# Turning the delta rows by a transposing DMA, with ScalarE's order and the first expert loads moved

## The reference, cut to what matters

```python
h = concat([meta, x])                                  # 4112 rows of 1024
u = rmsnorm(h, mix_norm)
proj = u @ w_in                                        # 3080 columns: xb, gb, q, k, v, z, beta, a
y_lru = rmsnorm(rglru(conv(xb)) * gelu(gb))            # 512 wide, a recurrence over the tokens
y_dn  = rmsnorm(gated_deltanet(q, k, v, beta, a)) * silu(z)   # 4 heads of 128, a recurrence over chunks
h = h + concat([y_lru, y_dn]) @ w_out
logits = rmsnorm(h, ffn_norm) @ router                 # top-1 of 4 groups, top-2 of its 8 experts
h = h + sum over the two chosen experts of gate * (silu(x @ w_gate) * (x @ w_up)) @ w_down
out = rmsnorm(h, final_norm)[16:]
```

## Time and profile before

| | |
|---|---|
| median of 3 runs | 3208.48 us (3200.05 to 3215.45) |
| the profiled execution | 3197.16 us, of which span 3195.5 us |
| TensorE busy | 2935.7 us (92% of the span) |
| VectorE, ScalarE, GpSimd busy | 2554.9, 1973.5, 907.7 us |
| mean granted TensorE clock | 0.969 of full speed |

### The profile page before, as it was taken

The page is one execution under the profiler, slowest core; times in us unless marked ns, Lnnn a source line. Parts: engine busy times, 40 slices in busy tenths (PEclk is TensorE's granted clock), DMA queues, the critical chain, the costliest instruction groups (busy, mean ns, idle before and its releaser), DMA issues. The chain is left out here.

```text
span 3195.5 us, 81737 instructions
## 1 busy us (share of the span) xinstructions
PE 2935.7 (92%) x28640; PEld 2195.9 (69%) x28641; DVE 2554.9 (80%) x7201; ACT 1973.5 (62%) x4385; POOL 907.7 (28%) x962
## 2 busy tenths in 40 slices
PE   4788999999999999999999999996799999999960
PEld 4777888788878887888788888874344555554530
DVE  6887888888878887888788878876788888888844
ACT  7554666565656566656555565653677777777746
POOL 4422222122212222221222122212344444444420
PEclk9999999999999999999999999998899999999985
DMA  6111232322222222222222222225487877777749
GB/s 231 65 37 32 70 100 72 86 71 75 74 87 68 81 74 81 68 81 76 79 74 74 82 73 80 70 72 211 119 275 223 239 211 199 193 222 217 230 99 394
DMA packets 186113, 396.53 MB, mean 124 GB/s; under 512 B 86992, under 2 KB 86992, under 8 KB 173520
## 3 DMA queue, kind: packets, MB, share of 16 engines
q1 hardware_dynamic: 148896, 286.22, 26.6%
q0 software_dynamic: 29216, 89.30, 12.2%
q10 hardware_dynamic: 7696, 16.86, 1.4%
HBM read 280.05 MB, written 96.01 MB: 118 GB/s over the span
## 5 line engine op out<-in xcount | busy, mean ns | idle before, releaser
L621 PE MATMUL pj<-uT,W 128*128 128x128 f16 x15744 | 974.4, 220 | 12.3 <-POOL W L1939 12.3
L621 PEld LDWEIGHTS pj<-uT,W 128*128 128x128 f16 x15744 | 927.0, 98 | 40.7 <-issue 30.4
L2295 DVE SCALAR_TENSOR_TENSOR W<-W,ecol 128x512 f16<-128x512 f16 x664 | 447.4, 746 | 111.0 <-ACT W L2239 103.1
L2239 ACT ACTIVATE W<-W,ecol 128x512 f16 x664 | 415.8, 708 | 79.2 <-issue 77.0
L2203 PE MATMUL bA<-W,uT 128*128 128x512 f16 x1992 | 447.1, 381 | 5.6 <-issue 4.4
L2203 PEld LDWEIGHTS bA<-W,uT 128*128 128x128 f16 x1992 | 193.6, 98 | 229.1 <-issue 10.0
L2187 PE MATMUL pj<-W,qs 128*128 x664 | 299.8, 594 | 0.9 <-ACT qs L2266 0.9
L2000 POOL TENSOR_TENSOR decb<-upto,nbeta 128x512 f32<-128x512 f16 x33 | 36.1, 1093 | 889.7 <-DVE nbeta L1735 889.7
L1025 ACT ACTIVATE ht<-ht 128x512 f32<-128x512 f32 x256 | 159.2, 623 | 95.2 <-DMA ht<-w_up 89.9
L2187 PEld LDWEIGHTS pj<-W,qs 128*128 128x128 f32 x664 | 119.9, 190 | 120.8 <-issue 120.2
L1055 ACT ACTIVATE qh<-bA 128x256 f32<-128x256 f32 x198 | 76.8, 388 | 191.4 <-PE bA L787 187.7
(11 more groups left out here) (508 smaller groups left out, 6119.8 us busy)
## 6 DMA issues: line engine op xcount, KB each, us to landing
ht<-w_gate SPq DMA_DIRECT2D x128, 256.0 KB, 3.1
ht<-w_up SPq DMA_DIRECT2D x128, 256.0 KB, 3.2
W<-w_gate SPq DMA_DIRECT2D x32, 1024.0 KB
W<-w_up SPq DMA_DIRECT2D x32, 1024.0 KB
W<-w_down SPq DMA_DIRECT2D x32, 1024.0 KB
x_in<-xm SPq DMA_DIRECT2D x33, 512.0 KB, 4.5
ht<-xm SPq DMA_DIRECT2D x32, 512.0 KB, 3.8
h_rows<-ht SPq DMA_DIRECT2D x32, 512.0 KB
```

Source lines behind the costliest of these rows:

```text
L621: mm = pe.matmul(pj[g % 2][:, j, :], w16[:, k, w_half(w_high, COL[GROUPS[g]], 512, j * P, P)], (ul if low_u else uh)[:, k, :], start=(k == ...
L2239: nc.scalar.activation(part_of(wx[par][:, 0], k), raw[:, k], ACT.Copy, scale=ecol[par][:, k:k + 1]).then_inc(sem("wx_high"), 1)
L2295: a = nc.vector.scalar_tensor_tensor(out=part_of(wx[par][:, 1], k), in0=raw[:, k], scalar=ecol[par][:, k:k + 1], in1=part_of(wx[par][:, 0] ...
```

## The change

The delta rows are split into halves before they are turned: ScalarE writes the high half from `yt` into `yd_rows`, a float16 view of the tile `ks`; VectorE the low half beside it; and one transposing DMA on SP's queue (`delta_columns`) turns both into `yd16`. TensorE's `turn_delta` is gone. VectorE waits for the DMA before the convolution of k overwrites `ks`. In steps with raw chunks the DMA stands ahead of chunk 2, elsewhere behind the `u_rows` store.

On ScalarE the copy of turned values moves ahead of the second norm's rsqrt and the evacuation of `xb`, and the square of chunk 1 (in steps 0 and 4, chunk 3) moves behind `level_y(s, 5)`. Step 32 now loads only expert 0; experts 1 to 3 are loaded in step 33.

```diff
+        yd_rows = ks[:].rearrange("p j n -> p (j n)").bitcast(F16)
...
# SP
                         for c in range(KT):
                             if c == KT - 2 and n == 1:
                                 turned_rows(s)
+                            if c == 2 and n == 0:
+                                delta_columns(s)
...
+                def delta_columns(s):
+                    if s.O:
+                        need(sp, sem("yd_ready"), s.nO)
+                        sp.dma_start(yd16.rearrange("p s j n -> p (s j) n"), yd_rows, transpose=True).then_inc(sem("yd_full"), 16)
...
                     raw_chunks(s)
+                    if not s.sums:
+                        delta_columns(s)
...
                             sp.wait_ge(sem("ba_full"), TILES)
-                            for slot in range(WSLOTS):
+                            load_expert(sp, 0, 0)
+                        if isinstance(s.i, int) and s.i == TILES:
+                            for slot in range(1, WSLOTS):
                                 load_expert(sp, slot, slot)
# TensorE
                         if j == 4:
-                            need(pe, sem("yd_ready"), s.nO)
+                            need(pe, sem("yd_full"), 16 * s.nO)
...
-                def turn_delta(s):
-                    need(pe, sem("yt_ready"), s.nO)
-                    need(pe, sem("kd_ready"), s.nG)
-                    for h in range(H):
-                        mm = pe.transpose(bT[:, h, :], yt[:, h, :], ident[:])
-                    mm.then_inc(sem("yd_full"), 1)
...
                     level_x(s, 3)
-                    if s.O and s.G:
-                        turn_delta(s)
...
-                        turn_delta(s)
                     late_part(s, 2)
                     if s.G:
                         need(pe, sem("X_new"), 6 * s.pG + 5)
-                        need(pe, sem("yd_ready"), s.nO)
+                        need(pe, sem("kd_ready"), s.nG)
# ScalarE
                         nc.scalar.activation(junk[:], ht[:], ACT.Square, accum_out=hst[:, 0:1]).then_inc(sem("h_stat"), 1)
+                    if s.G:
+                        need(act, sem("pre_full"), 5 * s.pG + 3)
+                        need(act, sem("vn_full"), s.pG)
+                        nc.scalar.activation(vt[:], bC[:], ACT.Copy).then_inc(sem("vt_ready"), 1)
+                    if s.R:
                         need(act, sem("h_stat"), 2 * s.pR + 1)
                         rsqrt(hst[:, 0:1], hst[:, 1:2], 1.0 / D, eps[:], ("h_stat", 2 * s.nR), "h_norm")
                     evac(s, 0, "xb")
                     if s.G:
-                        need(act, sem("pre_full"), 5 * s.pG + 3)
-                        need(act, sem("vn_full"), s.pG)
-                        nc.scalar.activation(vt[:], bC[:], ACT.Copy).then_inc(sem("vt_ready"), 1)
...
                     if s.O:
-                        need(act, sem("yd_full"), s.nO)
-                        nc.scalar.activation(yd16[:, 0], bT[:], ACT.Copy).then_inc(sem("yd_high"), 1)
+                        need(act, sem("yt_ready"), s.nO)
+                        nc.scalar.activation(yd_rows[:, 0:512], flat(yt), ACT.Copy).then_inc(sem("yd_high"), 1)
...
-                    if s.G:
-                        raw_squares(s, 1, twice=(3,))
                     level_y(s, 5)
                     if s.G:
-                        raw_squares(s, twice=(4,))
+                        raw_squares(s, 1, twice=(3, 4))
# VectorE
                     need(dve, sem("yd_high"), s.nO)
-                    nc.vector.tensor_tensor(yd16[:, 1], bT[:], yd16[:, 0], ALU.subtract).then_inc(sem("yd_ready"), 1)
+                    nc.vector.tensor_tensor(yd_rows[:, 512:1024], flat(yt), yd_rows[:, 0:512], ALU.subtract).then_inc(sem("yd_ready"), 1)
...
                     level_x(s, 6)
+                    if s.P:
+                        need(dve, sem("yd_full"), 16 * s.nO)
                     conv(s, 2, ks, 0, 1, 2, 3)
```

## The result

The changed kernel takes 3219.88 us (median of 7 runs, 3215.09 to 3225.53) where the kernel before takes 3204.39 us (7 runs, 3199.51 to 3215.45): the ratio is 1.004, 95% interval [1.0026, 1.0054]. That is 8 to 17 us more, where 8 us less was forecast; the forecast's median was 3201 and its widest range 3181 to 3215. The profiled execution has a span of 3218.4 us, 22.9 more than the one before.

What follows compares the result with a forecast made beforehand. TensorE's sequence of starts was taken to bound steps 3 to 31. Terms -12.2 - 8.4 - 8.1 + 5 + 16 = -7.7 us gave a 3201 us median; range 3188 to 3211, with rivals 3181 to 3215.

Steps and rivals of the forecast that it cites:

- step 4: ScalarE and TensorE wait as chunk 2 is loaded only after the delta rows: 5 us once, bounds 3 and 7.
- the three gains: TensorE's savings at the turned values, delta-row transposes and fifth level: 28.7 us together, about 0.95 a step, ends 18 and 34.
- Rival 2: In the levels the next wait replaces the removed ones; a step gains only 0.45 us: 3215 us, chance 0.10.
- `vt`: Ahead of `bC<-St,kh`: moving ScalarE's copy of turned values up removes 0.38 us in 32 steps, 12.2 us.
- The turn: At the fourth level: dropping TensorE's four delta-row transposes gains 0.28 us (0 to 0.44) in 30 steps, 8.4 us.
- the fifth level: Ahead of `level_x(5)`: chunk 1's square behind the evacuation saves TensorE 0.29 us in 28 steps, 8.1 us.
- The DMA in an ordinary step: Delta rows' copy lands 3.2 us after issue, at most 4.9, before VectorE's convolution of k: cost nothing.
- Rival 3: The copy lands after VectorE reaches the convolution of k; at 10 us it is +55, or 3263 us; chance 0.06.
- Step 33: In the drain `delta_columns` goes behind the `u_rows` store, so TensorE's columns come 2.5 us late.
- Step 34: The `h_rows` store waits behind nine expert loads on SP's queue, so `second_norm` starts 16 us later; bounds 2.5 and 19.
- Rival 1: The last `h_rows` store does not wait for the expert loads: the end costs 2.5 us, total 3187; chance 0.19.

Runs made afterwards that it cites:

- the split: Kernel after, plain DMAs for transposing ones, level 6's copy moved between the last two taps of q's convolution: 3163.86 us against 3184.71, step 62.22 us.
- its plain form: Kernel before with each transposing DMA replaced by a plain DMA of the same bytes: 3223.77 us, step 63.16 us.
- the late loads: Kernel after with plain DMAs, first loads of experts 1 to 3 issued behind the last step's `u_rows` store: 3179.12 us against 3184.71.

## Why the prediction was wrong

Between the medians' difference and the forecast's sum lie 15.5 - (-7.7) = 23 us: 17 from the steps, 1.5 from step 4 and the drain, 4.5 not placed. Point by point:

- **The step that failed** is the sentence "my sum of VectorE's work between the levels leaves it 0.1 to 0.5 us of slack at each", by which the three gains were added to 0.95 us a step. Each gain is right where it arises (0.38, 0.28 and 0.29 in the timeline). But at the copy of level 6 the slack was nil before any edit (the group ahead of the transposes of `X` 0.02 us over the measure), so the last two, 0.57 us, come back as the 0.58 us by which the group ahead of the transposes of `X` is over the measure. I had taken VectorE's durations as fixed; the taps went from 3.95 to 4.51 because GpSimd's group slid over the first of them. The gain was 10.2 us in 27 steps and 1.3 in the first four, against 28.7: 17 us of the error.
- **Rival 2** was the mechanism for the steps ("a step gains only 0.45 us", 3215): 0.33 was measured. It had a chance of 0.10; the earlier trace rows showed VectorE already last at the fourth level, and the copy behind the taps was not looked at.
- **`vt`**: right, 0.31 us by itself against 0.38.
- **The turn and the fifth level** are chained: the turn alone only lengthens the wait for ScalarE at the fifth level, the fifth level alone only that for VectorE. Neither gives anything alone, and together they give nothing without the split (62.85 with `vt` alone, 62.84 with all three) and 0.63 with it (62.85 to 62.22).
- **The DMA in an ordinary step** costs nothing: no wait of VectorE or TensorE for it in steps 3 to 31. It lands after 3.1 us, where I took 3.2. Rival 3 did not occur.
- **Step 4**: +6.1 against 5 less the step's gains. The chain was right in its links: chunk 2 is squared 8.3 us after the fourth level's evacuation (416.26 to 424.53), as worked out.
- **Step 33**: TensorE waits 2.4 us for the columns, 2.5 were forecast.
- **Step 34**: +16.4 us against 16. The store issued at 2231.40 landed after 18.4 us; I had it issued at 2231 and landed at 2250. Rival 1 falls. The 16 itself came out partly by estimates that no run shows by themselves: the 2 us of start-up and the 1 us for the receipt. The Trainium skill, page "DMA: Bandwidth & Descriptors", section "Two DMAs through the same engine are not ordered", has descriptors start in order within one queue of one engine; this landing and the 14 us that came back when the loads went behind the stores agree with it. What I had not seen is that the turn alone, with the loads left in step 32, costs 12 us there too.
- **The opening** was no term. It cost 5.0 us in the profiled execution, in a stretch that the change doesn't touch. TensorE's granted clock is 0.58 of full speed from 66 to 82 us, for the most part its lower level of 1.2 GHz, where the kernel before has 1.00; there the slow spell lies earlier and costs less (0.89 from 50 to 66 us, where the kernel after has 1.00; the 96 matmuls of a projection at 56.5 us take 7.16 us before and 5.53 after). After, TensorE was busy for 14.82 of the 16 us from 50 to 66 us, ahead of the fall. Over the profiles of all kernels step 0 starts at 124.9 us (before, its plain form, the turn alone, the late loads), 125.7, 126.6, 128.6 (twice), 129.7, 129.9 (three times), 130.3 and 131.0. None of the edits lies in this stretch, and the kernel with the late loads, which differs from the one after only in the drain, has 124.9 against 129.9 and 128.6. So no part of the change is its cause. It goes with where in the opening the clock falls: in the six profiles with a start of 126.6 us or less the granted clock is 1.00 from 66 to 82 us, in the others it falls there. Whether that is set anew in each execution, or partly by the program as a whole, two profiles of one kernel (1.3 us apart) don't tell. The opening may be part of the 4.5 us that are not placed.
- **The range**: it is said to follow from the ends of the terms, 3188 to 3211. The ends added (gains of 34 or 18, step 4 at 3 or 7, the drain at 2.5 or 19) give 3180 to 3216; the measured 3219.88 lies above that too.
- **Also open**: the 7.0 us between `second_norm` of step 34 and the end in these two executions. The kernel's work there is the same, and the spread of its runs (10 to 16 us) is larger; no experiment was made on it.

## What to carry to other kernels

When several waits are taken from the leading engine, don't add them up: walk the next engine's chain with the new start times, to the next instruction on which the leader waits, and look at which of its instructions the third engine's work will now lie beside. Where an instruction that the leader waits for stands behind a long helper job on its engine, splitting that job can be worth more than the waits removed upstream: here one moved line turned 0.33 us a step into 0.94. And a transfer put in a queue ahead of bulk loads, or bulk loads put ahead of a small store that something waits for, is paid for where nothing covers it: here 12 and 16 us of the drain.

## What the runs showed of the hardware

VectorE's `scalar_tensor_tensor` of 128 columns takes 0.34 us alone, and a string of them 0.29 us each. Where one of them starts while a `tensor_tensor` of GpSimd's runs, it does not end before GpSimd's does. In the stretch of the earlier trace rows there are 171 such cases in the two kernels together, and all but one end 0.14 to 0.15 us behind the GpSimd instruction beside which they started; the last one started 0.02 us ahead of GpSimd's next instruction and ended 0.15 us behind that one. An instruction of VectorE's that has run for 0.05 us or more when GpSimd's starts is not lengthened. GpSimd's own do not grow with the overlap (1.04, 1.29, 0.77 and 0.46 us after, within 0.01 us of those before). So the price is not a share of the overlap: the eight instructions lose 1.62 us in 2.69 us of overlap before and 2.18 in 3.26 after, and the 0.57 us of overlap added cost 0.56.

The Trainium skill, page "SBUF — State Buffer", section "Who interferes with whom", names the pair: a VectorE instruction with two SBUF inputs contends with a GpSimd instruction that reads SBUF. It calls the shared ports an exclusive lock. The trace agrees with both: the VectorE instruction is held to GpSimd's end, not slowed down in part.
